# First weight slab in quarters, a longer side list in the first gate block: a pooling and gated-linear-attention decoder step on eight cores

## What is computed

```python
h = _rmsnorm(x, g_mix)
u, q, k, v, og, zr, ga, gb = split(h @ w_in)
pool_out, new_buf = _pool_mix(u, ...)   # windows 2/4/8/16, minus token, per-group linear map
y_a = pool_out @ w_pool_proj
o, new_S = _gla(q, k, v, loga, S)       # gated linear attention, 4 heads, chunks
o = o * rsqrt(mean(o * o) + EPS) * g_gla_norm * silu(og)
y_b = o @ w_gla_proj
x = x + (sigmoid(ga) * y_a + sigmoid(gb) * y_b) @ w_out
gate, up = split(_rmsnorm(x, g_ffn) @ w_ffn_in)
x = x + (silu(gate) * up) @ w_ffn_out   # 2816 wide
```

## Time and profile before

| what | us |
|---|---|
| device time, median of 3 runs | 902.14 (901.99 to 902.38) |
| device time of the profiled execution | 901.29 |
| its span on the slowest core (core 0) | 900.2 |
| spans of the eight cores | 896.3 to 900.2 |
| TensorE busy | 875.1 (97%) |
| VectorE busy | 438.6 (49%) |
| ScalarE busy | 261.0 (29%) |
| GpSimd busy | 128.3 (14%) |

### The profile page before, as it was taken

The page is one execution under the profiler, slowest core; times in us unless marked ns, Lnnn a source line. Parts: engine busy times, 40 slices in busy tenths (PEclk is TensorE's granted clock), DMA queues, the critical chain, the costliest instruction groups (busy, mean ns, idle before and its releaser), DMA issues.

```text
span 900.2 us, 14507 instructions; the slowest of 8 cores (896.3 to 900.2 us)
## 1 busy us (share of the span) xinstructions
PE 875.1 (97%) x4888; PEld 447.7 (50%) x4888; DVE 438.6 (49%) x715; ACT 261.0 (29%) x515; POOL 128.3 (14%) x242
## 2 busy tenths in 40 slices
PE   4999999999999999999999999999999999999996
PEld 2544566654664566456644444444444444444443
DVE  4689565657435322433267664565651331232146
ACT  4563533223322123012226614332231011101123
POOL 4535112002100000100022001120120000000002
PEclk9999999999999999999999999999999999999999
DMA  8984842749709824943695994353774844352504
GB/s 208 219 167 78 118 75 38 127 98 157 129 24 180 171 34 84 166 92 68 110 173 171 214 203 72 59 90 44 132 114 62 135 88 68 55 113 47 94 24 164
DMA packets 57116, 100.50 MB, mean 112 GB/s; under 512 B 41538, under 2 KB 42178, under 8 KB 49748
## 3 DMA queue, kind: packets, MB, share of 16 engines
q0 software_dynamic: 10336, 66.75, 43.5%
q1 hardware_dynamic: 46564, 32.63, 15.3%
q10 hardware_dynamic: 144, 0.20, 0.1%
HBM read 139.36 MB, written 11.53 MB: 168 GB/s over the span
## 4 chain that ended last, share of the span: by engine, by line
PE 91%; DMA 4%; DVE 2%; issue 1%; ACT 1%; POOL 0%; DVEq 0%; POOLq 0%; ACTq 0%; SPq 0%
PE ps L422 87%; DMA ring<-w_f 1%; DMA ring<-w_a 1%; DVE R L319 1%; DMA R<-R 1%; PE ps L765 1%; PE ps L829 1%; DVE R L323 1%; DMA xres<-xm 0%; PE ps L407 0%; PE ps L746 0%; PE ps L766 0%; ACT R L315 0%; PE ps L540 0%; PE ps L723 0%
## 5 line engine op out<-in xcount | busy, mean ns | idle before, releaser
L422 PE MATMUL ps<-hT,ring 128*128 128x368 bf16 (+2 forms) x2720 | 506.5, 343 | 3.0 <-DVE qeZ L323 1.1
L422 PEld LDWEIGHTS ps<-hT,ring 128*128 128x128 bf16 x2720 | 260.5, 98 | 230.3 <-issue 7.9
L313 ACT ACTIVATE sgt<-ps 128x368 f32<-128x368 f32 (+2 forms) x207 | 109.6, 530 | 432.7 <-PE ps L422 381.2
L422 PE MATMUL ps<-ring,R 128*128 128x512 bf16 (+2 forms) x1028 | 222.5, 377 | 0.0
L319 DVE TENSOR_TENSOR R<-ps,sgt 128x368 bf16<-128x368 f32 (+1 forms) x110 | 66.1, 601 | 237.1 <-PE ps L422 229.7
L422 PEld LDWEIGHTS ps<-ring,R 128*128 128x128 bf16 (+1 forms) x1028 | 101.3, 99 | 118.3 <-issue 1.2
L319 DVE TENSOR_TENSOR xres<-xres,ps 128x512 f32<-128x512 f32 (+2 forms) x103 | 69.7, 680 | 66.2 <-PE ps L422 66.0
L422 PE MATMUL ps<-R,ring 128*128 128x368 bf16 (+1 forms) x320 | 70.6, 343 | 0.0
L315 ACT ACTIVATE R<-xres 128x1024 bf16<-128x1024 f32 (+3 forms) x45 | 45.8, 1018 | 83.3 <-DVE xres L323 43.4
L186 POOL DMA_DIRECT2D ring<-w_f x34 | 18.6, 549 | 294.4 <-PE ps L422 292.8
L422 PE MATMUL ps<-ring,hT 128*128 128x512 bf16 (+1 forms) x272 | 60.3, 379 | 0.0
(11 more groups left out here) (113 smaller groups left out, 443.9 us busy)
## 6 DMA issues: line engine op xcount, KB each, us to landing
ring<-w_f POOLq DMA_DIRECT2D x30, 1024.0 KB, 11.9
ring<-w_a POOLq DMA_DIRECT2D x24, 1024.0 KB, 12.3
y_p<-xres SPq DMA_DIRECT2D x15, 512.0 KB, 2.8
xres<-xp POOLq DMA_DIRECT2D x8, 512.0 KB, 12.3
R<-xp SPq DMA_DIRECT2D x8, 512.0 KB, 6.6
xres<-xp SPq DMA_DIRECT2D x8, 512.0 KB, 31.2
ring<-w_f POOLq DMA_DIRECT2D x4, 768.0 KB, 11.9
R<-sgla SPq DMA_DIRECT2D x2, 1024.0 KB, 10.6
```

The source lines that it names most:

```text
L313: T.op('act', lambda e: e.activation(out=out, in_=in_, func=func, scale=scale, bias=bias), reads=rd, writes=wr)
L422: return [(lambda e, k=k: e.matmul(out, lhsT=lw(k), rhs=rx(k), start=(k == 0), stop=(k == K - 1))) for k in range(K)]
```

## The change

- **Start.** Slab 0 is loaded as four DMAs of 1024 columns, between the x rows of units 1 to 3. The twelve warming matmuls become three behind each of the first three transpositions. The v projections of the first three units run quarter by quarter (`vq`). For later units `n1s` and `n1a` come one unit later. `loads` is reordered.
- **Order in `qk`.** k (tiles 2 and 3) is projected ahead of q (0 and 1), in both halves.
- **Pooling.** `windows('B', 2)` and `windows('B', 3)` leave the og stage and run operation by operation (`windows_g`, temporaries in `gfin_bc` and `gffn_bc`) within the first gate block X. `pool_mix('B', g)` moves from ahead of X to behind it, `pool_mix('S', g)` from Y to ahead of X. `load_gf`, which refills both temporaries, moves behind the windows. ScalarE writes the S columns of u to `sqb`, and GpSimd spreads them from there.
- **Side list.** In the first half `sR`, `sC` and `sD` of S come one step later.
- **FFN.** In the second half the first group's `seq` goes (0,0), (1,0), (0,1), (1,1).
- **End.** The last unit's sums go to columns of `gst` 8 apart, the later ones to `stat`.

```diff
...
         slabs += [('f', 0), ('f', 1), ('f', 2), ('g', 0), ('g', 1)] + [('f', j) for j in range(3, 15)]
-    sl = {'issued': 0, 'done': [False] * len(slabs), 'next': 0, 'limit': 1}
+    sl = {'issued': 0, 'done': [False] * len(slabs), 'next': 0, 'limit': 1, 'q': 0}
...
                 dst, src = ring[i][:, :], sgla.rearrange("p s c v -> p (s c v)")
+            if j == 0:
+                if sl['q'] < 4:
+                    q = sl['q']
+                    sl['q'] += 1
+                    T.dma('pool', f'd_rq{q}', [(dst[:, q * 1024:(q + 1) * 1024], src[:, q * 1024:(q + 1) * 1024])],
+                          writes=[dst[:, q * 1024:(q + 1) * 1024]])
+                sl['issued'] += sl['q'] == 4
+                break
...
     slab_topup()
-    for u in range(2, 4):
-        load_x(0, u, 'pool')
+    slab_topup()
+    load_x(0, 2, 'pool')
+    slab_topup()
...
         T.dma('pool', 'd_wpg', [(wpg_b[:, :], w_pg[:, :])], writes=[wpg_b[:, :]])
-    loads = {0: [lambda: load_x(0, 4, 'pool')], 1: [lambda: load_x(0, 5, 'pool')],
-             2: [lambda: load_x(0, 6, 'pool'), lambda: load_x(0, 7, 'pool'), load_cs, more_slab],
-             4: [load_hist], 5: [more_slab], 6: [load_wpg], 7: [more_slab]}
+    loads = {0: [lambda: load_x(0, 3, 'pool'), slab_topup], 1: [lambda: load_x(0, 4, 'pool'), lambda: load_x(0, 5, 'pool')],
+             2: [lambda: load_x(0, 6, 'pool'), lambda: load_x(0, 7, 'pool'), more_slab],
+             3: [load_cs], 4: [load_hist], 5: [more_slab], 6: [load_wpg], 7: [more_slab]}
...
             w = w8(rg)
-            for j in range(4):
+            for j in (2, 3, 0, 1):
...
 
-        def wsums(E, n, g):
-            ln = n - 1
-            a = wtmp[0][:, 0:ln]
-            tt(a, E[:, 1:n], E[:, 0:ln], ALU.add)
-            bi, sh = 0, 2
-            for lv in range(g):
-                ln -= sh
-                tt(wtmp[1 - bi][:, 0:ln], wtmp[bi][:, sh:sh + ln], wtmp[bi][:, 0:ln], ALU.add)
-                bi = 1 - bi
-                sh *= 2
-            return wtmp[bi][:, 0:ln]
-
-        def windows(blk, g):
+        def windows_g(blk, g, wt):
...
             E = Eb[:, g, e0:e0 + n]
-            ws = wsums(E, n, g)
+            ln = n - 1
+            tt(wt[0][:, 0:ln], E[:, 1:n], E[:, 0:ln], ALU.add)
+            yield
+            bi, sh = 0, 2
+            for lv in range(g):
+                ln -= sh
+                tt(wt[1 - bi][:, 0:ln], wt[bi][:, sh:sh + ln], wt[bi][:, 0:ln], ALU.add)
+                bi = 1 - bi
+                sh *= 2
+                yield
+            ws = wt[bi][:, 0:ln]
...
                 tt(pooled[:, g, SC + NS:SC + SR], mt, E[:, 15:31], ALU.subtract)
+            yield
+
+        def windows(blk, g):
+            for _ in windows_g(blk, g, wtmp):
+                pass
+
+        glate = [gfin_bc[:, 0:544], gffn_bc[:, 0:544]]
...
             E = xe[g]
+            us_ = sqb[:, g * NS:(g + 1) * NS].rearrange("p (s t) -> p s t", s=16)
+            T.op('pool', lambda e: e.tensor_copy(out=E[:, :, 15:19], in_=us_), reads=[us_], writes=[E[:, :, 15:19]])
...
                 act(Eb[:, g, 15:31], ps[:, NS:SR], AF.Copy)
-                act(xe[g][:, :, 15:19], ps[:, 0:NS].rearrange("p (s t) -> p s t", s=16), AF.Copy)
+                act(sqb[:, g * NS:(g + 1) * NS], ps[:, 0:NS], AF.Copy)
...
         if has_s:
-            j_v, rv = next_slab('a', 0)
+            j_v, rv = 0, ring[0]
+            sl['next'] = 1
...
             nb(0)
+            warm(3)
...
             nb(1)
+            warm(3)
...
             nb(2)
-            warm(12)
+            warm(3)
...
             n1a(3)
-            vp(0)
+            wv8 = w8(rv)
+            vb = [nbank() for _ in range(3)]
+
+            def vq(i, q):
+                c0, r, us = ucol(units[i])
+                out = banks[vb[i]][0:r, :]
+                pe([(lambda e, k=k: e.matmul(out, lhsT=hT[:, k, c0:c0 + r], rhs=wv8[:, k, :], start=(k == 0), stop=(k == 7)))
+                    for k in (2 * q, 2 * q + 1)], [rv[:, q * 1024:(q + 1) * 1024], hT[:, 2 * q:2 * q + 2, c0:c0 + r]], [banks[vb[i]][:, :]])
+            for q in range(3):
+                for i in range(3):
+                    vq(i, q)
+            nb(3)
...
             n1a(4)
-            vp(1)
-            nb(3)
-            n1s(6)
-            n1a(5)
-            vp(2)
+            for i in range(3):
+                c0, r, us = ucol(units[i])
+                vq(i, 3)
+                cpy(vTM[0:r, us, :], banks[vb[i]][0:r, :])
...
                 nb(i)
-                if i + 3 < 9:
-                    n1s(i + 3)
                 if i + 2 < 9:
-                    n1a(i + 2)
+                    n1s(i + 2)
+                if i + 1 < 9:
+                    n1a(i + 1)
...
             vp(8)
+            assert sl['q'] == 4
...
             pB[3]()
-            load_gf()
             j_og, rog = next_slab('a', 2)
-            og_all(rog, [lambda: windows('B', 2), lambda: windows('B', 3)])
+            og_all(rog, [])
...
                 sides.append(gl[t + 1][0])
-            if 1 <= t <= nU:
+            if has_s and t == 1:
+                sides.append(gl[0][2])
+            if 1 <= t <= nU and not (has_s and t == 1):
                 sides.append(gl[t - 1][3])
+            if has_s and t == 2:
+                sides.append(gl[0][3])
...
                 sides.append(gl[t][1])
-            if 1 <= t <= nU:
+            if has_s and t == 2:
+                sides.append(gl[0][4])
+            if 1 <= t <= nU and not (has_s and t == 1):
                 sides.append(gl[t - 1][4])
-            if t < nU:
+            if t < nU and not (has_s and t == 0):
...
             slab_release(j_qk)
-            for b_ in ['A', 'B']:
+            for b_ in (['A', 'S'] if has_s else ['A', 'B']):
...
             if has_s:
-                yield from gate('a', 0, r0, rp, cols[:1])
-                for i_, cost in enumerate(gate('a', 0, r0, rp, cols[1:2])):
-                    if i_ < 4:
-                        pool_mix('S', i_)
+                late = chain(windows_g('B', 2, glate), windows_g('B', 3, glate))
+                for cost in gate('a', 0, r0, rp, cols[:1]):
+                    next(late, None)
                     yield cost
-                yield from gate('a', 0, r0, rp, cols[2:])
+                for _ in late:
+                    pass
+                load_gf()
+                gflush()
+                for g in range(4):
+                    pool_mix('B', g)
+                    yield 0.22
+                yield from gate('a', 0, r0, rp, cols[1:])
...
             if nf < 8:
-                seq = [(0, 0), (1, 0), (0, 1), (1, 1), (2, 0), (2, 1)] if has_s else [(0, 0), (0, 1), (1, 0), (1, 1)]
+                seq = [(0, 0), (1, 0), (0, 1), (1, 1), (2, 0), (2, 1)] if has_s else [(0, 0), (1, 0), (0, 1), (1, 1)]
...
                 xt = xres[:, u, c0_:c0_ + n]
-                act(junk[:, c0_:c0_ + n], xt, AF.Square, scale=1.0 / 32.0, accum=gst[:, k:k + 1])
+                act(junk[:, c0_:c0_ + n], xt, AF.Square, scale=1.0 / 32.0, accum=gst[:, 8 * k:8 * k + 1])
...
             def final_l(u):
-                T.op('pool', lambda e: e.tensor_scalar(out=gst[:, 4:5], in0=gst[:, 0:1], scalar1=gst[:, 1:2], scalar2=EPS,
-                                                       op0=ALU.add, op1=ALU.add), reads=[gst[:, 0:2]], writes=[gst[:, 4:5]])
+                T.op('pool', lambda e: e.tensor_scalar(out=stat[:, 0:1], in0=gst[:, 0:1], scalar1=gst[:, 8:9], scalar2=EPS,
+                                                       op0=ALU.add, op1=ALU.add), reads=[gst[:, 0:1], gst[:, 8:9]], writes=[stat[:, 0:1]])
...
             def final_w(u):
-                T.op('pool', lambda e: e.tensor_scalar(out=gst[:, 5:6], in0=gst[:, 2:3], scalar1=gst[:, 4:5], scalar2=None, op0=ALU.add),
-                     reads=[gst[:, 2:3], gst[:, 4:5]], writes=[gst[:, 5:6]])
-                r_ = gst[:, 6:7]
-                tt(r_, gst[:, 5:6], negh[:, 0:1], ALU.pow, eng='pool')
+                T.op('pool', lambda e: e.tensor_scalar(out=stat[:, 8:9], in0=gst[:, 16:17], scalar1=stat[:, 0:1], scalar2=None, op0=ALU.add),
+                     reads=[gst[:, 16:17], stat[:, 0:1]], writes=[stat[:, 8:9]])
+                r_ = stat[:, 16:17]
+                tt(r_, stat[:, 8:9], negh[:, 0:1], ALU.pow, eng='pool')
```

1 line of the change is left out of this document (added).

## The result

The changed kernel takes 919.59 us, median of 4 runs (918.41 to 920.76), against 902.26 for the kernel before in the same comparison: a ratio of 1.019, with a 95% interval of 1.0171 to 1.0208. That is 17.3 us slower; the forecast was 2.2 slower and its range ended at 906.8. The profiled execution has 918.68.

The account below looks back on a forecast made before the run. TensorE, busy 875.1 of 900.2 us, was taken as the bound, so only its waits or clock count. Terms -1.3 + 5.0 + 0 - 1.0 - 0.5 = +2.2 gave 904.3 us against the median of 902.14; range 898.8 to 906.8.

Parts of the forecast that it names:

- FFN order: First FFN group of the second half: using the first two slabs for two blocks removes PE's 1.0 us slab wait, -1.0.
- og, q, k and first gate block: Og stage to first gate block: -1.65 for an earlier gate piece, +1.36 PE work, +5.3 waits; +5.0 in all.
- start: Start of the kernel: T3 3.15 us earlier, 0.44 less behind it, 2.3 given back in waits for norms; -1.3.
- k ahead of q, second half: Second half: the 1.4 us wait at L746 goes, but PE waits it again for ScalarE's pooling copies; 0 (-1.1 to +0.3).
- end: Last unit: ScalarE's 0.71 us wait for GpSimd, where the sums share a granule, goes; -0.5 (0 to -0.6).
- The main wait: First gate block: PE waits 3.4 us for PSUM bank 6, which VectorE's `ofb` of S alone frees.
- The first gate piece: Run-up to the first gate block: the piece at 98.49 comes 1.65 us earlier; the signs to look for said some 3.
- The last quarter: Start: the slab's last quarter is there by 21.4 and read at 21.7, just hidden, no cost.
- The norms' chain: Start: transposition, square and norm take 5.5 us for two units, so PE waits 1.15 ahead of T5 and T7, +2.3.
- The one on the other side (VectorE isn't the bound): Rival 1, first gate block: its 5.3 us of waits are absent, term -0.3, 899.0 us; chance 0.25.
- The fourth, the lock: Rival 4, first gate block: VectorE and GpSimd block each other, one meeting gives +1.5 net, 905.8 us; chance 0.08.

Follow-up runs that it names:

- the runs with the waits filled: Unused matmuls put where PE waits: in the second half's FFN of the changed kernel, 917.39 us; in the kernel before with the pooling part alone, 907.96 us.

## Why the prediction was wrong

By its own terms, with what the parts measured alone or by being taken back:

| term | forecast | measured |
|---|---|---|
| FFN order | -1.0 | +7.8 |
| og, q, k and first gate block | +5.0 | +7.5 |
| start | -1.3 | +1.6 |
| k ahead of q, second half | 0 | +0.8 |
| end | -0.5 | 0.0 |

They come to 17.7 for the 17.3 us, so nothing large is left unexplained. That they meet so closely is in part luck, as the start lost more alone than it did within the changed kernel (below).

**FFN: the step that failed.** I priced the wait for the third slab, 1.0 us, and said that using the first two slabs for two blocks removes it. It does, and with more to spare than the 7 us that I wrote: a block of 64 matmuls takes 13.8. I did not ask what the second block reads, so a wait for its input stood in my sum at nothing, without a reason. It reads the transposed columns of units 4 to 7, the last of which are issued as the FFN begins. The trace of the kernel before had the number (core 0, the last five transposing DMAs to `hT`, us to landing, least, median, greatest):

```profile
DMA to landing us min/median/max: 3.0/3.1/16.2
```

On the eight cores the greatest lay between 14.8 and 16.8 us, and it was that of the last one. On core 1 the last was issued at 666.6 and landed 14.9 later, at 681.5; block B came at 661.6 + 2 x 13.8 = 689.2, covered by 8 us. One block earlier it comes at 675.4, and the wait is 6.1 by that sum, against 6.24 measured. No rival of mine had it.

**Gate block and clock: the size that was off.** The main wait came out as written: at the output matmuls of L782 for `ofb`, 2.8 to 3.1 us against 3.4. Two smaller terms did not. The first gate piece came 0.7 to 2.1 us earlier over the cores, on core 0 at 97.27 for 98.49, where I had named some 3: ahead of it PE waits 2.2 us for ScalarE at the narrow pooling matmuls of S, which I had counted as work and not as waits. And behind L782 I had 1.9 us of waits for ScalarE's copies of B; there are none, and three cores wait 0.7 for VectorE there. These two nearly cancel, which is luck.

I summed all of them as idle time alone. The waits of rows 2 were too short to show what a longer one can do. Behind the 3.1 us, and behind the five waits of 0.4 to 0.7 in 3 us, PE ran at 1.2 GHz; the runs with the waits filled put that at 2.2 us in the block, and at 2.2 us in the FFN. The start rows had shown both levels, and I used them for the start alone.

**Start.** T3 came at 20.72 on core 0, for a forecast of 21.25, and at 21.59 on core 1 against its 23.87 before, as some of the 18 matmuls still ran at half rate there. The last quarter was waited for on some cores, 0.6 us on core 0. It landed between 20.8 and 22.2 us on the cores of the changed kernel, and at 22.6 on the worst of the run with the start alone: around my 21.4 and short of the 23 by the Trainium skill's 2.0 us for each DMA ("DMA: Bandwidth & Descriptors", Anatomy of one DMA). The norms' chain is what gave the gain back. Ahead of T5 PE waited 0.7 to 1.55 us in the changed kernel and ahead of T7 1.45 to 1.65, for a forecast of 1.15 each, and there was a third wait ahead of T4, up to 0.9, that I had not: the chain starts from an x row that is later than before, and I had let x rows arrive as before. The v projection ended 0.7 us later on core 0. In the run with the start alone the wait ahead of T5 reached 2.6 us, the lower clock came on top on cores 0 and 1, and v ended 3.3 us later on core 0. That is why this part lost 1.6 us alone.

**Second half and end.** The pooling copies did hide what was won, as forecast; that the k transpositions themselves become slower (10.5 for 7.0 us to landing on core 1) I had within my upper bound of +0.3 only, and the +0.8 measured for it is within the noise. At the end I took the 0.71 of ScalarE's wait as the limit, where GpSimd stood behind VectorE's norm.

**Rivals.** The one on the other side (VectorE isn't the bound) needed PE to pass the block without a wait, which it didn't. The fourth, the lock, shows at the end of the kernel and in og. In the block it cost VectorE nothing: each of its window additions there took 0.69 to 0.70 us on core 1.
